# Both down projections of the decoder trunk as seven block products, the first one's weight sums built by transfers

## The chip, the core and the metric

The kernel runs on one core of a Trainium2 chip. The time is the device time of one execution in microseconds (us). Three runs of the kernel before took 1356.61, 1356.44 and 1354.90 us, median 1356.44. The profiled execution took 1356.42 us.

## What is computed

A decoder trunk of two layers on 512 positions of width 1024, float32. Layer 0 mixes with a convolution and a gated part, layer 1 with dilated attention over 3 x 8 heads. Each layer ends with a feed-forward part. Every matrix product is made of three: both operands are split into a high and a low float32r part, and high x high, high x low and low x high are summed.

```python
def swiglu(x, w_gate, w_up, w_down):
    return (jax.nn.silu(x @ w_gate) * (x @ w_up)) @ w_down
...
        x = layer_norm(DN_ALPHA * x + swiglu(x, ffn_w_gate[layer], ffn_w_up[layer], ffn_w_down[layer]),
                       ln_g[layer, 1], ln_b[layer, 1])
```

The hidden width is 2816, or 22 tiles of 128. The change is in the last product, 512 x 2816 by 2816 x 1024.

## The kernel before, in words

**Stages.** Layer 0: convolution part (0 to 158 us), up projection (158 to 384.5), down projection (384.5 to 506). Layer 1: attention (506 to 1012), up projection (to 1240), down projection (to 1345.5), last norm. The queues of the five engines are written out by hand, and semaphores are waited for in that order.

**Slabs.** Weights come in slabs of 128 x 1024 floats (512 KB). SyncE (SP) loads slab s into slot s % 4 of `stage` (L598) once the low part of slab s - 4 is made. ScalarE (ACT) rounds it to `w_hi` (`split_high`, L1401) once TensorE (PE) has used slab s - 4. GpSimd (POOL, `split_low`, L707) or VectorE (DVE, `low_slab`, L2323) makes `w_lo`, and PE follows.

**Up projections.** The last 20 hidden tiles ("units") are made by seven half-size products in place of eight. Each unit takes a slab of gate and a slab of up weights. DVE adds blocks of them (`sum31` L2239, `sum2` L2248, `sum4` L2254) and makes all low parts. The up slab of unit n is loaded (SP L649) once DVE has made the low part of the last operand of the unit two before (`low_d`, L2282), and `sum31` waits for it. The unit's turn ends with `corner_12` (L2301), the Silu on ACT (L1655) and `unit_hidden` (L2309), which writes a row of `ht`. POOL has nothing to do here.

**Down projection of layer 0.** Plain: 22 slabs, each 4 token tiles x 2 halves x 3 matmuls of 512 columns, 528 in all (L846 to L848). ACT splits weights and `ht` rows (`high_ht`, L1664), POOL makes the weights' low part, DVE the rows' (`low_ht`, L2316). Between them DVE works out the rotary angles (`rotary_angles` 0 to 3, behind rows 8 to 11, in the tile `gate`), and ACT the sine and cosine tables (`rotary_tables`, L1572, behind row 14). PE ends with `finish_tiles`, which goes tile by tile over the last three slabs, so that the norm of tile 0 begins three tiles before the end.

**Down projection of layer 1.** By blocks (`down_by_blocks`). The 22 hidden tiles are 11 pairs. For each pair PE does four products of 6 matmuls with two prepared slabs from DRAM (`t_rows`: 22 slabs), then with two plain slabs, six slabs of "four" sums (five whole, one half), and nine plain ones: 264 + 132 + 66 = 462 matmuls. DVE makes sums and low parts (`sums_of` L2335 and L2338, `fourth_sum`, `low_sums` L2350, `low_own` L2356, `low_row`, `corners`). The norm of tiles 0 and 1 begins behind the "four" slabs, with the last six plain slabs put between its steps (`between`).

**Sums of weights.** `t_rows` is built in DRAM during attention. Behind every fourth slab SP copies three pieces per pair (`copy_blocks`, 1.25 MB), and POOL issues four accumulating transfers per pair (`block_sums`: step 0 L782, 1 L785, 2 L789, 3 L792), one behind each `split_low`.

**Seam.** `norm` (ACT L1422, L1427, L1435; DVE L1943, L1963; POOL `add_shift` L715) makes x of each tile, PE turns it (`turn_x`, L860), ACT and DVE split it, and the next stage's columns begin (`columns_behind_norm`). The lines that the change touches stand below.

Of the kernel before, what the change touches and what calls it, by code (L numbers as in the profile page):

```python
# [7 lines left out]
F32 = mybir.dt.float32  # L8
# [3 lines left out]
ALU = mybir.AluOpType  # L12
# [31 lines left out]
N_IN, N_OUT, N_UP, N_DOWN, N_ATT = 16, 8, 2 * KF, KF, 72  # L44
# [8 lines left out]


PAIRS = KF // 2
FRONT_ROWS = 2
SUM4_SLABS = (PAIRS + 1) // 2
S_REST = S_DOWN1 + 2 * PAIRS
S_SUM4 = S_REST + FRONT_ROWS
S_ROWS = S_SUM4 + SUM4_SLABS  # L60
N_SLABS = S_ROWS + PAIRS - FRONT_ROWS
OP_SLOTS = 4
# [14 lines left out]
HT_RING = 9  # L77
# [38 lines left out]
def trunk(nc, x, positions, ev_w_in, ev_conv_w, ev_conv_b, ev_conv_ln_g, ev_conv_ln_b, ev_sgu_ln_g,  # L116
# [3 lines left out]
    with ctx:  # L120
# [49 lines left out]
        with ExitStack() as s:  # L170
# [13 lines left out]
            def ht_rows(k):  # L184

                slot = k % HT_RING
                if slot < HT_FIRST:
                    return hr_hi[:, slot, :], hr_lo[:, slot, :]
                n, half = divmod(slot - HT_FIRST, 2)
                chunks = slice(2 * half, 2 * half + 2)  # L190
                return tuple(t[:, n, chunks, :].rearrange("p k n -> p (k n)") for t in (xs_hi, xs_lo))

# [27 lines left out]
            rot_tmp = gate[:, 0, :].rearrange("p (n t) -> p n t", n=4)  # L220
            pos_i = ones[:, :].bitcast(I32)
        with ExitStack() as s:
# [22 lines left out]
            t_rows = nc.dram_tensor("t_rows", (2 * PAIRS + SUM4_SLABS, P, SLAB), F32, kind="Internal").ap()  # L245
# [103 lines left out]
        t_copied = sem("t_copied")  # L349
        t_two = sem("t_two")  # L350
        t_three = sem("t_three")
        t_four = sem("t_four")
        h_sum_set = sem("h_sum_set")
        h_four_set = sem("h_four_set")
        op_hi_set = sem("op_hi_set")
        op_lo_set = sem("op_lo_set")
        m_done = sem("m_done")
        m_kept_set = sem("m_kept_set")
        corner_set = sem("corner_set")
# [160 lines left out]

        def row_blocks(slab):

            if S_SUM4 <= slab < S_ROWS:
                q = slab - S_SUM4
                return ht[:, 4 * q + 1:min(4 * q + 4, KF):2, 0:HALF]
            return pair_blocks(row_pair(slab))[:, 0:4:3, :]

        def slab_width(slab):  # L530

            return SLAB // 2 if slab == S_ROWS - 1 else SLAB

        def row_pair(slab):

            return slab - S_REST if slab < S_SUM4 else slab - S_ROWS + FRONT_ROWS

        def slab_view(slab):
# [31 lines left out]
            if S_DOWN0 <= slab < S_ATT:  # L570
                return rows(ffn_w_down[0], slab - S_DOWN0)
# [2109 lines left out]
```

## Time and profile before

| what | value |
|---|---|
| median of 3 runs | 1356.44 us |
| profiled execution | 1356.42 us, span of instructions 1354.6 us |
| PE busy | 1341.0 us (99%) |
| DVE busy | 940.1 us (69%) |
| ACT busy | 642.9 us (47%) |
| POOL busy | 435.1 us (32%) |
| granted clock of PE | 0.997 of full speed |
| moved by DMA | 176.23 MB, mean 130 GB/s |

Busy time and idle time are told apart by semaphore events. Matmuls are pipelined: one of 512 columns is shown as 0.39 us long, and the next starts 0.23 us behind it, so the time of a stage is the number of matmuls by that step, plus stalls. The 1.8 us between execution and span lie before the first and behind the last instruction.

### The profile page before, as it was taken

To read this page: it belongs to the slowest core of one execution; us is meant where nothing else is said; L and a number is where in the kernel's file an instruction comes from. 1 tells how busy PE (TensorE), PEld (TensorE's weight loads), DVE (VectorE), ACT (ScalarE), POOL (GpSimd) and SP (SyncE) were. 2 spreads that over 40 slices of the span, in tenths; PEclk is the share of its full clock that TensorE was granted. 3 is DMA by queue.
4 is the path that set the end of the run, shared out by engine and by line. 5 is a ranking of instruction groups with operands and counts; after the bars stand their busy time and mean duration, and the time that the engine had idled before them with its cause. 6 is when DMAs were issued, how large, how long until landed. Compare 5 with 4: busy or idle time off the path is not lost.

```text
span 1354.6 us, 20715 instructions
## 1 busy us (share of the span) xinstructions
PE 1341.0 (99%) x8055; PEld 1195.8 (88%) x8055; DVE 940.1 (69%) x1219; ACT 642.9 (47%) x997; POOL 435.1 (32%) x240
## 2 busy tenths in 40 slices
PE   8999999999999999999999999999999999999997
PEld 7887899999988889888888888888889999999885
DVE  3997598888866456777542767644238888889977
ACT  4465555554543343333422334333446455556566
POOL 4785600000054445555544535354242000000002
PEclk9999999999999999999999999999999999999999
DMA  9322224334353325777375776545222434335653
GB/s 272 93 95 85 71 68 120 93 102 115 95 176 105 94 62 162 193 189 187 95 218 147 178 191 164 130 142 148 55 62 76 112 93 113 103 93 202 202 181 123
DMA packets 197083, 176.23 MB, mean 130 GB/s; under 512 B 10293, under 2 KB 163657, under 8 KB 196840
## 3 DMA queue, kind: packets, MB, share of 16 engines
q1 hardware_dynamic: 182648, 156.59, 38.7%
q0 software_dynamic: 7744, 14.42, 6.1%
q10 hardware_dynamic: 6624, 4.29, 1.3%
q8 instruction: 45, 0.74, 0.2%
q14 instruction: 22, 0.18, 0.0%
HBM read 171.04 MB, written 33.08 MB: 151 GB/s over the span
## 4 chain that ended last, share of the span: by engine, by line
PE 97%; ACT 1%; DVE 1%; DMA 1%; issue 0%; SPq 0%; DVEq 0%; ACTq 0%
PE pq L1135 10%; PE pq L1134 10%; PE pq L1132 10%; PE pq L824 9%; PE pq L825 9%; PE pq L826 9%; PE pq L846 8%; PE pq L847 8%; PE pq L848 8%; PE pq L1330 3%; PE pq L1328 3%; PE pq L1329 3%; PE pq L1307 1%; PE pq L1266 1%; PE pq L1279 1%; PE pq L1300 1%
## 5 line engine op out<-in xcount | busy, mean ns | idle before, releaser
L707 POOL TENSOR_TENSOR w_lo<-stage,w_hi 128x1024 fp32r<-128x1024 f32 x132 | 327.0, 2482 | 573.5 <-ACT w_hi L1401 573.5
L1401 ACT ACTIVATE w_hi<-stage 128x1024 fp32r<-128x1024 f32 x173 | 179.1, 1053 | 199.4 <-PE pq L848 126.3
L824 PE MATMUL pq<-xt_hi,w_hi 128*128 128x512 f32 (+1 forms) x624 | 228.4, 366 | 0.5 <-DVE xt_lo L1930 0.4
L826 PE MATMUL pq<-xt_hi,w_lo 128*128 128x512 f32 (+1 forms) x624 | 225.2, 361 | 0.0
L825 PE MATMUL pq<-xt_lo,w_hi 128*128 128x512 f32 (+1 forms) x624 | 225.2, 361 | 0.0
L1134 PE MATMUL pq<-xt_lo,w_hi 128*128 128x256 f32 x632 | 178.9, 283 | 0.0
L1135 PE MATMUL pq<-xt_hi,w_lo 128*128 128x256 f32 x632 | 178.9, 283 | 0.0
L1132 PE MATMUL pq<-xt_hi,w_hi 128*128 128x256 f32 x632 | 178.8, 283 | 0.0
L715 POOL TENSOR_TENSOR x_res<-x_res,norm_b 128x512 f32<-128x512 f32 x24 | 30.4, 1292 | 338.7 <-ACT x_res L1435 337.2
L824 PEld LDWEIGHTS pq<-xt_hi,w_hi 128*128 128x128 f32 x624 | 117.9, 189 | 19.6 <-DVE xt_lo L1930 1.2
L826 PEld LDWEIGHTS pq<-xt_hi,w_lo 128*128 128x128 f32 x624 | 117.8, 189 | 18.0
L1132 PE MATMUL pq<-xs_hi,w_hi 128*128 128x256 f32 x472 | 133.6, 283 | 0.0
L1134 PE MATMUL pq<-xs_lo,w_hi 128*128 128x256 f32 x472 | 133.6, 283 | 0.0
L1135 PE MATMUL pq<-xs_hi,w_lo 128*128 128x256 f32 x472 | 133.6, 283 | 0.0
L825 PEld LDWEIGHTS pq<-xt_lo,w_hi 128*128 128x128 f32 x624 | 117.9, 189 | 17.1
L1132 PEld LDWEIGHTS pq<-xt_hi,w_hi 128*128 128x128 f32 x632 | 121.3, 192 | 0.1
L1134 PEld LDWEIGHTS pq<-xt_lo,w_hi 128*128 128x128 f32 x632 | 121.3, 192 | 0.1
L1135 PEld LDWEIGHTS pq<-xt_hi,w_lo 128*128 128x128 f32 x632 | 121.3, 192 | 0.0
L1132 PEld LDWEIGHTS pq<-xs_hi,w_hi 128*128 128x128 f32 x472 | 90.6, 192 | 0.0
L1134 PEld LDWEIGHTS pq<-xs_lo,w_hi 128*128 128x128 f32 x472 | 90.6, 192 | 0.0
L1135 PEld LDWEIGHTS pq<-xs_hi,w_lo 128*128 128x128 f32 x472 | 90.6, 192 | 0.0
L2540 DVE TENSOR_TENSOR qk<-qk,norm_g 32x1024 f32<-32x1024 f32 x24 | 85.6, 3566 | 0.8
(287 smaller groups left out, 2915.7 us busy)
## 6 DMA issues: line engine op xcount, KB each, us to landing
stage<-in_od_w_qkv_dram SPq DMA_DIRECT2D x72, 512.0 KB, 4.4
stage<-in_ffn_w_gate_dram SPq DMA_DIRECT2D x44, 512.0 KB, 4.9
stage<-in_ffn_w_up_dram SPq DMA_DIRECT2D x44, 512.0 KB, 4.0
stage<-in_ffn_w_down_dram SPq DMA_DIRECT2D x33, 512.0 KB, 3.5
stage<-t_rows SPq DMA_DIRECT2D x27, 512.0 KB, 3.3
t_rows<-in_ffn_w_down_dram SPq DMA_DIRECT2D x22, 512.0 KB, 7.4
stage<-in_ev_w_in_dram SPq DMA_DIRECT2D x16, 512.0 KB, 5.5
t_rows<-in_ffn_w_down_dram POOLq DMA_DIRECT2D x11, 512.0 KB, 7.9
```

The costliest lines, as they stand in the source:

```text
L707: pool.tensor_tensor(w_lo[slab % RING][:, :], w_stage[slab % RING][:, :], w_hi[slab % RING][:, :].bitcast(F32), ALU.subtract).then_inc(w_l ...
L824: pe.matmul(o, hi[:, k, :], x_hi, start=(k == 0), stop=False)
L825: pe.matmul(o, hi[:, k, :], x_lo, start=False, stop=False)
L826: last = pe.matmul(o, lo[:, k, :], x_hi, start=False, stop=(k == KD - 1))
L846: pe.matmul(o, t_hi[:, tile * P:(tile + 1) * P], hi, start=first, stop=False, skip_group_check=resumed)
L847: pe.matmul(o, t_hi[:, tile * P:(tile + 1) * P], lo, start=False, stop=False, skip_group_check=resumed)
L848: return pe.matmul(o, t_lo[:, tile * P:(tile + 1) * P], hi, start=False, stop=end, skip_group_check=resumed)
L1132: pe.matmul(o, hi[:, k, :], x_block[0][:, k, :], start=(first and k == 0), stop=False, skip_group_check=True)
L1134: pe.matmul(o, hi[:, k, :], x_block[1][:, k, :], start=False, stop=False, skip_group_check=True)
L1135: last = pe.matmul(o, lo[:, k, :], x_block[0][:, k, :], start=False, stop=(k == KH - 1), skip_group_check=True)
L1401: act.activation(w_hi[slab % RING][:, 0:width], w_stage[slab % RING][:, 0:width], ACT.Copy).then_inc(w_hi_ready, 1)
L2540: dve.tensor_tensor(rows, rows, rot[0:ROT, :, :], ALU.add).then_inc(qk_set, 1)
```

## The change

The down projection of layer 0 goes by `down_by_blocks` too, with 462 matmuls in place of 528. Semaphores of the scheme get a copy per layer, and so does `t_rows`. Its copies stand on SP behind slabs 8 to 23 of the convolution part, its accumulating transfers on POOL behind slabs 17 to 23 and then two per unit of the up projection. The "four" sums take seven slabs (four whole, three half) in both layers. POOL makes no low parts in layer 0's down projection, DVE makes all. The rotary work moves: angles behind pairs 5 and 9 and behind the third and sixth "four" slab, tables behind the second of the last nine slabs, in a tile of their own (`rot_tmp`). In the norm, `split(0)` moves behind `between(1)`.

```diff
+SUM4_WHOLE = 4
+SUM4_SLABS = PAIRS - SUM4_WHOLE
+SUMS_FROM = 16
+COPY_BEHIND = (8, 9, 11, 12, 14, 15, 17, 18, 20, 21, 23)
...
+            def copy_blocks(layer, j):
+
+                upper, lower, both, own, four = block_rows(layer, j)
+                if j >= 2:
+                    sp.wait_ge(t_copied[layer][j % 2], 48 * (j // 2))
...
             for slab in range(RING + 4, S_UP0):
                 load(slab)
+                if slab in COPY_BEHIND:
+                    copy_blocks(0, COPY_BEHIND.index(slab))
...
+            def load_down(first, layer, e):
+                for n in range(N_DOWN):
+                    if n == 2:
+                        load_ln(e, layer, 1)
+                    if n < D_REST and n % 2 == 0:
+                        sp.wait_ge(t_three[layer], 16 * (n // 2 + 1))
+                    elif n == D_SUM4:
+                        sp.wait_ge(t_four[layer], 16 * PAIRS)
+                    load(first + n)
...
+            sums_begun = 0
             for slab in range(S_UP0):
                 split_low(slab)
+                if slab >= SUMS_FROM:
+                    block_sums(0, sums_begun)
+                    sums_begun += 1
                 if slab == 17:
                     pool.wait_ge(acc_set, 1)
...
-            feed_forward(S_DOWN0, 1)
+            for u in range(UNITS):
+                pool.wait_ge(s31_set, min(u + 2, UNITS))
+                for _ in range(2):
+                    if sums_begun < 4 * PAIRS + 4:
+                        block_sums(0, sums_begun)
+                        sums_begun += 1
+            pool.wait_ge(w_lo_ready, plain(S_ATT))
+            norm(1, S_ATT)
...
                         if r:
                             last.then_inc(w_used, 1)
+                            if layer == 0 and slab < end_slab - 1:
+                                turn_x(2, slab - end_slab + 3)
...
-                split(0)
+                if not between:
+                    split(0)
                 squares_of(0)
...
                 if between:
                     between(1)
+                    split(0)
                     scale(0)
...
+                for slab in range(fours, row_slabs + 4):
+                    high_row(slab)
+                    if layer == 0 and slab == row_slabs + 1:
                         rotary_tables()
...
+                        if layer == 0 and j in (5, 9):
+                            rotary_angles(j // 9)
...
+                        if layer == 0 and slab - fours in (2, 5):
+                            rotary_angles(2 + (slab - fours) // 5)
```

**How the queues change.** POOL in the convolution part, slabs 16 to 18. `tap_sum` and `acc` are the partial and whole sums of the convolution, `L707` and `L730` the low part of a slab. Before:

```order
L755 TENSOR_TENSOR tap_sum<-tap_sum,mixed 128x512 x2
L707 TENSOR_TENSOR w_lo<-stage,w_hi 128x1024
L747 TENSOR_TENSOR tap_sum<-acc 128x512
L755 TENSOR_TENSOR tap_sum<-tap_sum,mixed 128x512 x2
L760 TENSOR_TENSOR acc<-acc,tap_sum 128x512
```

Now:

```order
L730 TENSOR_TENSOR w_lo<-stage,w_hi 128x1024
L778 DMA t_rows<-in_ffn_w_down_dram 256x1x512
L796 TENSOR_TENSOR tap_sum<-acc 128x512
L804 TENSOR_TENSOR tap_sum<-tap_sum,mixed 128x512 x2
L809 TENSOR_TENSOR acc<-acc,tap_sum 128x512
L730 TENSOR_TENSOR w_lo<-stage,w_hi 128x1024
L782 DMA t_rows<-in_ffn_w_down_dram 128x512
```

A transfer of step 1 is issued ahead of the last sums of the convolution.

ACT at the end of layer 0's down projection. Rows that write `w_hi` split a weight slab, rows that write `hr_hi` or `xs_hi` its partner from `ht`. The rows `ht,sq_sum` and `std` are the norm's squares and root, `x_res` its scaled tile. Before:

```order
L1401 ACTIVATE w_hi<-stage 128x1024
L1422 ACTIVATE ht,sq_sum<-pq,neg_mean 128x1024
L1427 ACT_TABLE_LOAD
L1427 ACTIVATE std<-sq_sum,eps 128x1
L1435 ACTIVATE x_res<-pq,rstd 128x512 x2
```

Now:

```order
L1594 ACTIVATE sin_t<-rot_tmp 32x128 x4
L1594 ACTIVATE cos_t<-rot_tmp 32x128 x4
L1421 ACTIVATE w_hi<-stage 128x1024
L1709 ACTIVATE hr_hi<-ht 128x512
L1421 ACTIVATE w_hi<-stage 128x1024
L1709 ACTIVATE xs_hi<-ht 128x512
L1442 ACTIVATE ht,sq_sum<-pq,neg_mean 128x1024
L1447 ACT_TABLE_LOAD
L1447 ACTIVATE std<-sq_sum,eps 128x1
L1421 ACTIVATE w_hi<-stage 128x1024
L1709 ACTIVATE xs_hi<-ht 128x512
```

Behind these come the second tile's squares, three more pairs of splits, one more `w_hi`, and only then `x_res`. The tables stand seven slabs before the end, where there was nothing of them.

DVE at pair 5 of layer 0's down projection. `w_lo<-stage` is `low_slab`, the rows from `sums` and `ht` into `xs_lo` are `low_sums` and `low_own`. Now:

```order
L2313 TENSOR_TENSOR w_lo<-stage,w_hi 128x1024
L2340 TENSOR_TENSOR xs_lo<-sums,xs_hi 128x768
L2346 TENSOR_TENSOR xs_lo<-ht,xs_hi 128x256
L2148 CAST rot_tmp<-ones 128x128
L2150 TENSOR_SCALAR rot_tmp<-rot_tmp,cst 128x128
L2134 TENSOR_SCALAR rot_tmp<-rot_tmp 128x128
L2136 TENSOR_SCALAR rot_tmp<-rot_tmp 128x128
L2138 TENSOR_SCALAR rot_tmp<-rot_tmp 128x128
L2142 SCALAR_TENSOR_TENSOR rot_tmp<-rot_tmp 128x128 x3
L2155 TENSOR_SCALAR rot_tmp<-rot_tmp 128x128
L2313 TENSOR_TENSOR w_lo<-stage,w_hi 128x1024
```

In layer 1's block version the last row follows `low_own` at once.

## Rows read from the trace of the kernel before

**Rows 1.** The page, its part on the chain that ended last, by engine
```profile
PE 97%; ACT 1%; DVE 1%; DMA 1%; issue 0%; SPq 0%; DVEq 0%; ACTq 0%
```

**Rows 2.** Busy time by stretch; columns: stretch, length, PE, PEld, DVE, ACT, POOL, clock, DMA
```profile
384.50:506.10 121.60, 121.58 (x544) 100.39 (x543) 65.37 (x74) 45.87 (x67) 55.94 (x25) 1.00 0.31 96
...
1240.00:1345.50 105.50, 105.44 (x464) 86.25 (x462) 91.33 (x128) 67.49 (x93) 4.34 (x4) 1.00 0.52 173
```

**Rows 3.** Timeline of PE; columns: start, length, engine, line, operation, idle before
```profile
499.28 0.39 PE L846 MATMUL pq<-w_hi,xs_hi 128*128 128x512 f32 x1
...
501.09 0.39 PE L848 MATMUL pq<-w_hi,hr_lo 128*128 128x512 f32 x1
...
506.24 0.36 PE L824 MATMUL pq<-xt_hi,w_hi 128*128 128x256 f32 x1 [0.16 <-issue]
...
1345.19 0.39 PE L848 MATMUL pq<-w_hi,xs_lo 128*128 128x512 f32 x1
```

**Rows 4.** Timeline of DVE, layer 0's down projection (415 to 419) and layer 1's
```profile
415.83 0.21 DVE L2153 CAST gate<-ones 128x128 f32<-128x128 int32 x1
...
418.17 0.23 DVE L2160 TENSOR_SCALAR gate<-gate 128x128 f32<-128x128 f32 x1
...
1265.50 0.42 DVE L2356 TENSOR_TENSOR xs_lo<-ht,xs_hi 128x256 fp32r<-128x256 f32 x1
...
1270.02 0.95 DVE L2350 TENSOR_TENSOR xs_lo<-sums,xs_hi 128x768 fp32r<-128x768 f32 x1
```

**Rows 5.** Timeline of ACT, layer 0's tables and layer 1's last rows
```profile
450.86 1.73 ACT L1572 ACTIVATE sin_t<-gate 32x128 f32<-32x128 f32 x4
...
1319.84 1.06 ACT L1401 ACTIVATE w_hi<-stage 128x1024 fp32r<-128x1024 f32 x1 [1.14 <-PE pq L848]
...
1326.90 1.04 ACT L1401 ACTIVATE w_hi<-stage 128x1024 fp32r<-128x1024 f32 x1
```

**Rows 6.** Timeline of POOL, PE and DVE at the two norms
```profile
489.12 2.40 POOL L707 TENSOR_TENSOR w_lo<-stage,w_hi 128x1024 fp32r<-128x1024 f32 x1 [3.03 <-ACT w_hi L1401]
497.45 2.55 POOL L715 TENSOR_TENSOR x_res<-x_res,norm_b 128x512 f32<-128x512 f32 x2 [5.93 <-ACT x_res L1435]
...
501.32 1.03 PE L860 MATMUL pq<-ident,x_res 128*128 128x128 f32 x8
...
1338.95 1.28 DVE L1963 SCALAR_TENSOR_TENSOR pq<-pq,neg_mean,norm_g 128x1024 f32<-128x1024 f32 x1
```

**Rows 7.** Timeline of POOL and PE in the convolution part
```profile
103.36 1.30 POOL L747 TENSOR_TENSOR tap_sum<-acc 128x512 f32<-128x512 f32 x1
...
107.48 1.27 POOL L760 TENSOR_TENSOR acc<-acc,tap_sum 128x512 f32<-128x512 f32 x1
...
107.94 1.99 PE L965 MATMUL pq<-acc,ones 128*128 128x512 f32 x4
```

**Rows 8.** Timeline of SP, DVE and ACT, one unit of layer 0's up projection
```profile
251.83 0.37 SPq L649 DMA_DIRECT2D stage<-in_ffn_w_up_dram  x1
...
255.85 1.22 DVE L2239 TENSOR_TENSOR sums<-stage 128x1024 f32<-128x1024 f32 x1
...
258.27 0.63 ACT L1655 ACTIVATE gate<-gate 128x512 f32<-128x512 f32 x1 [1.51 <-DVE gate L2301]
...
259.46 0.69 DVE L2309 TENSOR_TENSOR ht<-pq,gate 128x512 f32 x1 [1.22 <-PE pq L1135]
```

**Rows 9.** Slab loads (L598) of attention issued at 599.4, then at 635.5
```profile
DMA to landing us min/median/max: 5.1/5.1/5.1
...
DMA to landing us min/median/max: 4.2/4.2/4.2
```

**Rows 10.** Timeline of POOL and DVE in attention
```profile
596.75 2.65 POOL L707 TENSOR_TENSOR w_lo<-stage,w_hi 128x1024 fp32r<-128x1024 f32 x1
599.09 1.32 POOL L785 DMA_DIRECT2D t_rows<-in_ffn_w_down_dram  x1
...
596.79 3.70 DVE L2540 TENSOR_TENSOR qk<-qk,norm_g 32x1024 f32<-32x1024 f32 x1
```

More of the change, by code:

```diff
@@ L76 @@
 HT_FIRST = 3
-HT_RING = 9
 C_FAR, C_NEAR, C_UT, C_FREQ, C_SIGN = 0, 256, 640, 768, 769
@@ L650, in load_up @@
                                      gate_up[j % 2][:, :, 2 * t + j // 2, :]).then_inc(w_loaded[slot], 16)
-            def load_down(first, layer, e, end):
-                if layer:
-                    sp.wait_ge(t_four, 16 * PAIRS)
-                load(first)
-                load(first + 1)
-                load_ln(e, layer, 1)
-                for slab in range(first + 2, end):
-                    load(slab)
+            def load_down(first, layer, e):
[7 more added lines that the diff above has]
+                    load(first + n)
             load_up(S_UP0, 0)
@@ L1774, in feed_forward @@
-                high_ht(1)
                 split_high(down + 1)
                 split_high(down + 2)
-                high_ht(2)
                 unit_gate(last, last % 2)
+                high_sums(1)
+                high_own(1)
                 split_high(down + 3)
-                for k in range(HT_FIRST, KF):
-                    high_ht(k)
-                    if RING <= k + 1 < KF:
-                        split_high(down + k + 1)
-                    if layer == 0 and k == 14:
+                for j in range(2, PAIRS):
+                    split_high(down + 2 * j)
+                    split_high(down + 2 * j + 1)
+                    high_sums(j)
+                    high_own(j)
@@ new lines, in feed_forward @@
+                for slab in range(rest, fours):
+                    high_row(slab)
+                for n, (dst, bank) in enumerate(((sums, 1), (gate, 5))):
+                    act.wait_ge(m_done[layer], n + 1)
+                    for r in range(2):
+                        last = act.activation(dst[:, r, :], pq[:, bank + 2 * r, :], ACT.Copy)
+                    last.then_inc(m_kept_set[layer], 1)
+                for slab in range(fours, row_slabs + 4):
+                    high_row(slab)
+                    if layer == 0 and slab == row_slabs + 1:
@@ L1785, in feed_forward, with between @@
                         rotary_tables()
-                norm(e, down + N_DOWN)
+                def between(n):
+                    for slab in ((row_slabs + 4, row_slabs + 5), range(row_slabs + 6, end_slab))[n]:
+                        high_row(slab)
+                norm(e, down + N_DOWN, between)
             feed_forward(0, S_UP0, S_DOWN0, 1)
@@ L2445, in unit_step @@
                         sum2(u + 2, par)
-                    elif layer:
+                    else:
                         sums_of(0)
-                        low_slab(S_DOWN1)
+                        low_slab(down)
                         low_sums(0)
-                    else:
-                        low_d(u + 1, 1 - par, static + 1)
-                        low_ht(0)
                     corner_12(u, par)
-                    if layer and not more:
+                    if not more:
                         low_d(u + 1, 1 - par, static + 1)
@@ L2484, in feed_forward @@
                     unit_step(u, u % 2, u)
[L2485 to L2500 removed]
+                down_by_blocks()
+            feed_forward(0, S_UP0, S_DOWN0, 1)
             def stream_tables():
```

374 lines of the change are left out of this document (154 added, 220 removed).

## The prediction

> **What bounds the kernel now.** I read the chain that ended last first. It lies on PE for 97% [rows 1]. The table by stretch says the same of both down projections: PE is busy 121.58 of 121.60 us in layer 0 (with its seam) and 105.44 of 105.50 in layer 1, at full clock [rows 2]. So a matmul taken away shortens the time, as long as nothing else comes late. What may come late is read from timelines of the other queues, each against the moment at which PE needs the result. The steps of PE are 0.2265 us, (501.09 - 499.28) / 8 [rows 3].
>
> The sum is made against the profiled execution, 1356.42 us. The median of the three runs is 1356.44, so the two stand together. No change means within 0.2%, or 2.7 us.
>
> **Term 1, matmuls: -15.0.** 528 become 462, 66 x 0.2265 = 14.95 us. Nothing else on PE is taken away. The turns of tiles 0 and 1 stay.
>
> **Term 2, the usual small stalls: +0.4.** Layer 1's block version runs from 1240.0 to 1345.19 + 0.23 = 1345.42 [rows 2, 3], 105.4 us for 462 steps of 104.6, so 0.8 of stalls. The plain version had 121.74 (384.5 to 506.24) less 119.6 less 1.8 for the turns, 0.3. The difference is 0.4 to 0.5.
>
> **Term 3, rotary angles on DVE: +0.3 (0 to 2.5).** DVE now makes all low parts. In layer 1 a pair takes it 4.87 us (steps of 1.14 twice, 0.87, 0.72 and 0.33 three times) of PE's 5.44, so it gains 0.57 per pair until ACT holds it. Part 0 takes 2.57 us, 415.83 to 418.17 + 0.23 [rows 4]. Put behind pair 5 (`low_own` ends at 1265.9), it moves pair 6's `low_sums` from 1270.97 to about 1273.1. PE wants pair 6 at 1240.4 + 6 x 5.44 = 1273.0. With 0.15 us from DVE to PE that is a stall of 0.3. Part 1 (2.05) comes when 1.6 of lead is won back, and pair 10 has no next sum, so it is hidden. Parts 2 and 3 (2.25 each) find 1 us of lead or more. Without any lead each part would be paid in full for a slab, hence 2.5.
>
> **Term 4, the tables on ACT: +3.3 (0 to 5).** Sine and cosine are two times 1.73 us [rows 5]. Before, ACT had two splits, about 1.6 us, against the 24 steps or 5.44 us that PE took for a slab there, and the gaps hid them. Call the nine plain slabs at the end p0 to p8. In layer 1 ACT begins p2 at 1319.84, waiting for PE, and p4 at 1326.90, behind the first squares [rows 5]. PE needs p4 at 1345.4 less 36 steps less two slabs of 2.72, 1331.8, and the split takes 2.9 to be ready on DVE, so there are 1.9 us of room. Now p1 starts at 1318.4 (three half slabs let PE free its slot 1.3 later), then 1.5 for p1 and 3.5 for the tables: p2 at 1323.4, 3.6 late. The norm's first sum on DVE, the squares and the table load for the root follow, and p4 begins at 1330.9, 4.0 late against 1.9 of room. Rolled on to p8 by the same durations, PE waits 0.3, 0.4, 1.4, 0.4, 0.1, 0.4 and 0.4, together 3.3. The lower end is zero (another 2 us of room somewhere), the upper one 3.5 and the second squares.
>
> **Term 5, the seam: +2.7 (0 to 5).** Before, the adds of tile 0 end at 497.45 + 2.55 = 500.0, and PE turns it at 501.32, 1.3 later [rows 6]. Now tile 0's gain stands behind the low parts of p8, as at 1338.95 in layer 1, 6.5 us before the end [rows 6]. Count from R, the end of p8's low parts. PE has 12 matmuls until the first turn, R + 2.9. The chain is the last rotary step 0.45, gain 1.2, scale 0.7, then POOL. But POOL has `split_low` of attention's first slab first, 2.4 us [rows 6], to about R + 3.0, and two adds, 2.55, bring it to R + 5.5. PE can turn the first half meanwhile. It waits 2.0 at tile 0, 0.3 at tile 1 and 0.4 at the first columns. The lower end is the old seam, the upper one both tiles in full.
>
> **Term 6, the convolution part: +1.1 (0 to 1.3).** POOL's last sums run without a gap from 103.36, and the last one ends at 107.48 + 1.27 = 108.75. PE takes two `ones` matmuls in 107.94 to 109.86, so the second starts at 108.9, just behind it [rows 7]. A transfer of step 1 now stands ahead of these sums. POOL spends 1.32 us on one such beside DVE work [rows 10]. I take 1.1, and 0 if POOL had unseen room. The later six transfers fall where POOL idles. The eleven copies on SP stand ahead of slab loads that PE wants only three slabs later, 3 x 24 steps or 16 us, which covers a load that has to queue.
>
> **Term 7, layer 0's up projection: +3.3 (0 to 15).** POOL idles here, but two accumulating transfers per unit now share the DMA engines with the slab loads, and one load stands in a loop with no depth. The up slab is issued at 251.83 and `sums` starts at 255.85, 4.0 later; the Silu ends at 258.27 + 0.63 = 258.9; the hidden row could start at 259.0 and starts at 259.46, held by PE [rows 8]. The room is 0.45 us per unit of 10.08 (84 steps of half size, 0.12 each). In attention a slab load issued beside steps 0 and 1 landed after 5.1 us, and one beside steps 2 and 3 after 4.2 [rows 9], against 4.0. So units take turns at +1.1 and +0.2: 0.65 over the room, then 0.25 won back, 0.4 per two units. Nine pairs give 3.6, less 0.3 before PE feels it. If transfers add under 0.45 everywhere it is 0. The upper end is the rival below.
>
> The skill states a mechanism for the same sharing. The Trainium skill, DMA: Bandwidth & Descriptors, section SWDGE vs HWDGE vs iDMA, says that inside each DMA engine transfers issued by GpSimd and by SP lie in different queues, and that the engine takes turns between them. By that rule a load beside a steady accumulate could take up to twice its transfer time, which is the strong case below, and the 5.1 us say it is milder.
>
> **Term 8, layer 1: +0.5 (0 to 1).** Seven "four" slabs in place of six delay the last rows by 0.3, and the last norm, which ended 0.7 behind PE, by 0.2 more.
>
> **Hidden:** the new splits of DVE (POOL's former ones), by the idle time that layer 1 shows: 91.33 of 105.50 busy [rows 2]. The start of the down projection: it is layer 1's queue, and the sums of pair 0 are there 100 us earlier.
>
> **Sum:** -15.0 + 0.4 + 0.3 + 3.3 + 2.7 + 1.1 + 3.3 + 0.5 = -3.4, and 1356.4 - 3.4 = **1353.0 us**. Own range of this case 1349 to 1356.5.
>
> **Rivals.**
>
> *A, most of it is kept.* Layer 1's twin runs with 0.8 us of stalls, so terms 4, 5 and 7 might shrink to little. With all three at 0 the time is 1343.7, with each at a half 1348.4. For it speaks rows 2, against it the queue positions worked out above.
>
> *B, the load loop decides, slower.* Place: the up slab's load between `low_d` and `sum31`. If the load takes 1.5 us more beside steps 0 and 1 and 0.6 beside 2 and 3, two units cost 1.05 + 0.15, nine pairs 10.8, term 7 is 10.5 and the time 1360.2; with 1.8 and 0.9 it is 1365.6. It decides from a mean of about 1.0 us added per load (term 7 over 9.4). For it: our transfers are already in flow when the load starts, 3 to 4 us behind their issue, and two follow at once. Against it: 5.1 and 4.2 [rows 9].
>
> *C, POOL's issuing holds DVE.* 1.32 + 0.8 us per unit against 1.6 of idle time on DVE would cost 0.5 per unit, 10 us in all, on top of the sum: 1363. Against it speaks attention: the split of POOL runs from 596.75 to 599.40, the DVE operation beside it ends at 596.79 + 3.70 = 600.49, 1.1 after the split, though the transfer is being issued in just that time (599.09 to 600.41) [rows 10]. So the split holds DVE, the issue doesn't. The Trainium skill, SBUF — State Buffer, section Who interferes with whom, says that a DVE instruction with two SBUF inputs contends with a GpSimd one that reads SBUF, and not with one that only writes. By that rule, the trace agrees.
>
> *D, a wait on `t_three` or `t_four` stops the loads.* The last sums are issued a unit before the end and land within 8 us; the first slab needs only pair 0. Its price would be a landing, 8 us.
>
> **How the numbers follow.** Forecast 0.45 (faster 0.27, same 0.14, slower 0.04), A 0.28 (all faster), B 0.18 (slower 0.12, same 0.06), C 0.04 (slower), D 0.05 (same). Faster 0.55, same 0.25, slower 0.20, with C, D and both tails rounded. The range 1344.5 to 1361 leaves out the best of A and the worst of B and C.
>
> **What the profile after would show.** Right: 66 fewer matmuls of 512 columns; PE with gaps of a few tenths to 1.4 us in the last six slabs of layer 0's down projection, released by DVE low parts; about 2 us at the first turn, released by POOL; about 1 us ahead of the last `ones` matmul; units of 10.2 to 10.4 us in place of 10.08 in layer 0 alone. Wrong: units still 10.08 (A) or over 10.6 (B); DVE operations in the units longer than 1.22 and 0.69 (C); a gap of several us at the start of the down projection (D).

## The result, and the profile after

The changed kernel is slower: 1374.24 us against 1356.44, ratio 1.0133 (95% interval 1.0104 to 1.0162). The forecast was 1353.0, range 1344.5 to 1361. The profiled execution took 1373.06 us with a span of 1371.0, 16.4 more than before.

The page of the changed kernel has this for the chain that ended last, by engine, which answers to [rows 1]:

```profile
PE 79%; DMA 5%; DVE 5%; POOL 4%; issue 4%; ACT 2%; DVEq 0%; SPq 0%; POOLq 0%; ACTq 0%
```

PE had 97% of the chain before and has 79% now. What is new in it is told by its list of longest pieces (start, length, what):

```profile
200.86 4.70 DMA stage<-in_ffn_w_up_dram
211.26 6.24 DMA stage<-in_ffn_w_up_dram
...
234.31 7.09 DMA stage<-in_ffn_w_up_dram
...
507.10 2.53 DVE sin_t L2175
```

These are slab loads of layer 0's up projection, of about 4 us before, and the rotary sign product at the seam. The table by stretch (columns as in [rows 2]) has the up projection, one piece of it, and layer 0's down projection with its seam:

```profile
182.30:403.90 221.60, 208.34 (x1682) 206.41 (x1681) 167.94 (x223) 108.32 (x163) 33.62 (x38) 0.98 0.72 157
337.00:340.40 3.40, 3.40 (x16) 3.40 (x17) 3.24 (x4) 1.77 (x4) 0.00 (x0) 0.52 0.96 122
403.90:520.50 116.60, 111.25 (x480) 88.46 (x478) 103.17 (x167) 73.86 (x108) 7.73 (x5) 0.99 0.53 177
```

The same matmuls, 84 per unit in 20 units, took 201.6 us before, at a DMA share of 0.40. PE is idle in this stretch for 13.3 us, and in places its clock is granted at half. From starts of matmuls in both timelines the 16.4 us come out as follows:

| stretch | before | after | difference |
|---|---|---|---|
| start, to the first columns | 16.53 | 14.88 | -1.65 |
| first columns to the first unit | 166.21 | 167.39 | +1.18 |
| layer 0's up projection | 201.59 | 221.61 | +20.02 |
| its down projection, seam and columns, to attention's first product | 152.37 | 147.11 | -5.26 |
| attention to layer 1's up projection | 501.70 | 501.67 | 0.0 |
| layer 1's up projection | 201.60 | 201.59 | 0.0 |
| layer 1's down projection, to the last matmul | 105.19 | 105.31 | +0.1 |
| behind the last matmul | 9.41 | 11.44 | +2.03 |

The first row is scatter as far as is known: this start took 14.5 to 17.1 us in the profiles of the changed kernel and its variants, and 16.6 in a second one of the kernel before.

So the products were saved where they should be, and the up projection gave back more than all of it. The waits of that stretch, longest of each kind:

```profile
DVE sums L2235 <- DMA stage<-in_ffn_w_up_dram: 26.2, 16, 3.5
...
PE pq L1164 <- DVE ht L2305: 13.3, 9, 2.4
```

The first difference of a unit (`sum31`) waits for the up slab's load in 16 units, the hidden row is late behind it, and PE stands in nine of them. What such a stand costs is seen in PE's timeline:

```profile
242.65 0.28 PE L1167 MATMUL pq<-xt_hi,w_lo 128*128 128x256 f32 x1
245.38 0.58 PE L1164 MATMUL pq<-xt_hi,w_hi 128*128 128x256 f32 x1 [2.45 <-DVE ht L2305]
245.75 0.42 PE L1166 MATMUL pq<-xt_lo,w_hi 128*128 128x256 f32 x1
245.97 0.42 PE L1167 MATMUL pq<-xt_hi,w_lo 128*128 128x256 f32 x1
```

The next start comes 2.73 us later in place of 0.12, and then the steps are 0.21 for some 3 us. The row of the stretch at 337.0 above shows the same behind another such gap: granted clock 0.52, that is the lower level of 1.2 GHz. The nine gaps add up to 14.7 us beyond a step, and the slow steps behind them to 5.3, mostly behind three gaps of 2.3 to 2.6 us: the 20 us.

### The profile page after: what moved, and what is told of

Read it like the earlier page. It is cut to its first block, busy times and chain, and to the rows that moved or that the text cites. A ratio compares the mean times of both kernels' runs of the same rounds, so it can differ in the third digit from the quotient of the medians.

```text
span 1371.0 us, 20908 instructions
## 1 busy us (share of the span) xinstructions
PE 1336.6 (97%) x7989; PEld 1187.5 (87%) x7989; DVE 986.4 (72%) x1320; ACT 669.3 (49%) x1039; POOL 417.7 (30%) x262
## 3 DMA queue, kind: packets, MB, share of 16 engines
q1 hardware_dynamic: 190312, 179.67, 43.1%
## 4 chain that ended last, share of the span: by engine, by line
PE 79%; DMA 5%; DVE 5%; POOL 4%; issue 4%; ACT 2%; DVEq 0%; SPq 0%; POOLq 0%; ACTq 0%
PE pq L850 8%; PE pq L852 8%; PE pq L851 8%; PE pq L1164 7%; PE pq L1166 7%; PE pq L1167 7%; PE pq L872 6%; PE pq L874 6%; PE pq L873 6%; DMA stage<-in_ffn_w_up_dram 5%; PE pq L1348 3%; PE pq L1350 3%; PE pq L1349 3%; POOL tap_sum L804 2%; POOL w_lo L730 1%
## 5 line engine op out<-in xcount | busy, mean ns | idle before, releaser
L730 POOL TENSOR_TENSOR w_lo<-stage,w_hi 128x1024 fp32r<-128x1024 f32 x110 | 271.4, 2472 | 419.6 <-ACT w_hi L1421 306.8
L1421 ACT ACTIVATE w_hi<-stage 128x1024 fp32r<-128x1024 f32 (+1 forms) x192 | 197.1, 1042 | 163.7 <-PE pq L874 88.1
L1164 PE MATMUL pq<-xt_hi,w_hi 128*128 128x256 f32 x632 | 182.0, 288 | 13.3 <-DVE ht L2305 13.3
L851 PEld LDWEIGHTS pq<-xt_lo,w_hi 128*128 128x128 f32 x624 | 117.9, 189 | 17.1
L2313 DVE TENSOR_TENSOR w_lo<-stage,w_hi 128x1024 fp32r<-128x1024 f32 (+1 forms) x80 | 94.5, 1181 | 18.1 <-ACT w_hi L1421 17.6
L872 PE MATMUL pq<-w_hi,xs_hi 128*128 128x512 f32 x228 | 90.4, 396 | 1.5 <-DVE xs_lo L2357 0.9
```

The costliest lines, as they stand in the source:

```text
L730: pool.tensor_tensor(w_lo[slab % RING][:, :], w_stage[slab % RING][:, :], w_hi[slab % RING][:, :].bitcast(F32), ALU.subtract).then_inc(w_l ...
L851: pe.matmul(o, hi[:, k, :], x_lo, start=False, stop=False)
L872: pe.matmul(o, t_hi[:, tile * P:(tile + 1) * P], hi, start=first, stop=False, skip_group_check=resumed)
L1164: pe.matmul(o, hi[:, k, :], x_block[0][:, k, :], start=(first and k == 0), stop=False, skip_group_check=True)
L1421: act.activation(w_hi[slab % RING][:, 0:width], w_stage[slab % RING][:, 0:width], ACT.Copy).then_inc(w_hi_ready, 1)
L2313: dve.tensor_tensor(w_lo[slab % RING][:, 0:width], w_stage[slab % RING][:, 0:width], w_hi[slab % RING][:, 0:width].bitcast(F32), ALU.subtr ...
```

## The experiments

All ratios stand against the kernel before, measured on the same chip as the run (1354.7 to 1355.1 us there; 1356.4 where the change was measured). Stretches are of the one profiled execution. In runs 1, 2 and 5 sums of weights stay unfinished, so the slabs' waits for them are left out in runs 1 and 2.

**1. No transfers in the up projection.** My first theory was the forecast's rival B: transfers and loads share the DMA engines.

```diff
-            for u in range(UNITS):
-                pool.wait_ge(s31_set, min(u + 2, UNITS))
-                for _ in range(2):
-                    if sums_begun < 4 * PAIRS + 4:
-                        block_sums(0, sums_begun)
-                        sums_begun += 1
...
+                    if layer == 0 and n == 0:
...
+                        sp.wait_ge(t_two[0], 64)
...
```

> Leaves out the 40 accumulating transfers of the first layer's up projection (its weight sums stay unfinished, so the output is another one); the 8 places in the convolution part, all copies and the whole down projection stay as in the changed kernel. The load theory (the transfers share the DMA engines with the two 512 KB loads of each unit, the loads land late, PE idles 14.7 us at the units' ends and runs some 5 us longer at half clock after the longest of these gaps) expects the up stretch back at 201.6 us instead of 221.6 and 1354.2 us in all, ratio to the kernel before 0.998. The rival, that the loss sits in the down projection and the norm behind it and the up stretch is only where it shows in one profile, expects less than 5 us back: 1369 or more.

Measured: 1352.82 us, ratio 0.9982 (0.9973 to 0.9992), up stretch 201.59. The whole loss of that stretch hangs on these transfers.

**2. One small transfer per unit, at the same point.**

```diff
-                for _ in range(2):
-                    if sums_begun < 4 * PAIRS + 4:
-                        block_sums(0, sums_begun)
-                        sums_begun += 1
+                if u < 18:
+                    upper, _, _, own, _ = block_rows(0, 2 + u // 2)
+                    at = slice(512 * (u % 2), 512 * (u % 2) + 512)
+                    pool.dma_start(own[:, at], upper[:, at], accum_op=ALU.add).then_inc(t_three[0], 16)
```

> In each of 18 units of the first up projection one accumulating transfer of 256 KB in place of two of 256 and 512 KB (the others are left out, so sums stay unfinished and the output is another one), issued at the same point, where the unit's first difference is done. The load theory: 256 KB land about 5.2 us after the issue, the next loads are issued 4.3 us after it, so the transfer is nearly out of their way: up stretch 201.6 to 204, 1354 to 1357 us in all. A rival, that it is POOL's issuing (0.8 to 1.1 us each, beside DVE's operations) which makes DVE late and the loop long, keeps half of the loss with half of the issues: up stretch about 211, total about 1364.

Measured: 1352.62 us, 0.9987 (0.9977 to 0.9997), up stretch 201.59. Half the issues cost nothing, so POOL's issuing as such is not it. This run changes both the number of issues and the bytes; it is the next that changes neither.

**3. The transfers together with the loads.**

```diff
-                pool.wait_ge(s31_set, min(u + 2, UNITS))
+                pool.wait_ge(d_lo_set, u + 1)
```

> All transfers as in the changed kernel, but POOL waits for the unit's d split instead of its first difference, so that both transfers of a unit are issued together with its two loads and not 4.3 us ahead of them. The load theory expects a worse kernel: every load now runs beside a fresh 512 to 768 KB, landings of 7 us and more in every unit instead of some, up stretch 230 to 250 us, total 1382 to 1403. If only the volume counts, or the issuing, the stretch stays at 221 and the total at 1374.

Measured: 1353.34 us, 0.9994 (0.9985 to 1.0004), up stretch 201.59. My theory was wrong in its core: with every transfer kept, and every load beside them, the loss is gone. Volume alone doesn't decide either; the DMA share of this stretch is 0.73 and PE is never idle:

```profile
181.90:383.50 201.60, 201.60 (x1682) 201.60 (x1681) 168.03 (x223) 108.36 (x162) 33.56 (x38) 1.00 0.73 170
```

The rows of the large transfer of step 1 (L778) and of the up slab's load behind or ahead of it (L679) say why. First of the changed kernel, where the load goes out 3.6 us behind the transfer:

```profile
L778 POOL DMA_DIRECT2D t_rows<-in_ffn_w_down_dram x1: 1370/1370/1370, 207.7 to 207.7; - x1
DMA to landing us min/median/max: 8.1/8.1/8.1
...
L679 SPq DMA_DIRECT2D stage<-in_ffn_w_up_dram x1: 373/373/373, 211.3 to 211.3; - x1
DMA to landing us min/median/max: 6.2/6.2/6.2
```

Then of run 3, where it goes out 0.8 us ahead of it (and 0.3 us ahead of the smaller transfer of step 0):

```profile
L778 POOL DMA_DIRECT2D t_rows<-in_ffn_w_down_dram x1: 1367/1367/1367, 211.4 to 211.4; - x1
DMA to landing us min/median/max: 9.5/9.5/9.5
...
L679 SPq DMA_DIRECT2D stage<-in_ffn_w_up_dram x1: 373/373/373, 210.7 to 210.7; - x1
DMA to landing us min/median/max: 4.1/4.1/4.1
```

The load lands as if alone, and the transfer is the one to wait, 9.5 us in place of 8.1. It ends at 220.9, when the next up load is just going out (220.7). The second load of the pair, issued 0.6 to 0.9 us behind the first, now lands after 6.8 to 8.8 us, and before after 5.0; it is wanted later, and PE never waits for it.

The two queues, from run 3's view of 210.5 to 214 us, show what the 0.3 us are worth (packets, MB, share of the 16 engines; `hardware_dynamic` are SP's transfers, `software_dynamic` POOL's):

```profile
q1 hardware_dynamic: 1144, 0.58, 56.5%
q0 software_dynamic: 1, 0.00, 0.3%
```

More than a whole slab of 512 KB has passed while POOL's transfers, issued at 210.9 and 211.4, have moved one packet.

**4. The transfers just ahead of the loads.** New theory: who comes first. Its opponent: only the amount left in flight counts.

```diff
-                pool.wait_ge(s31_set, min(u + 2, UNITS))
+                pool.wait_ge(hid_set, u + 2)
```

> All transfers as in the changed kernel; POOL waits for the unit's hidden product, so that they go out about 1.4 us ahead of the next unit's load, where the changed kernel sends them 4.3 us ahead and the run at the loads 0.3 us behind it. The run at the loads took the loss away (up stretch 201.59 us), against my first theory of shared engines. Theory of who comes first: a load that finds transfers in the queues ahead of it is late, one that leads them lands as if alone. It expects the load to land after 6 us or more in every unit and an up stretch of 221 to 245, total 1373 to 1397. Theory of the tail: the load only shares with what is left of transfers, and POOL's start and descriptors take some 2 us first, so that 1.4 us ahead is as good as together: up stretch 201.6 to 206, total 1353 to 1358.

Measured: 1414.77 us, 1.0443 (1.0425 to 1.0460), up stretch 260.99. The same transfers, 1.7 us earlier relative to the load than in run 3, cost 59 us. The unit loads of both slabs together (L679) from 190 to 400 us, in the changed kernel, in run 3 and in run 4 (who waited for them: total us and times; then their landings):

```profile
  DVE sums L2235: 26.2, 16
...
DMA to landing us min/median/max: 4.0/5.4/7.9
```

```profile
  DVE sums L2235: 1.2, 5
...
DMA to landing us min/median/max: 3.8/4.1/8.8
```

```profile
  DVE sums L2235: 51.8, 16
...
DMA to landing us min/median/max: 6.4/8.0/9.3
```

For the up slab alone, which is the one that `sum31` waits for, the medians are 4.0 us in the kernel before, 5.3 in the change, 3.9 in run 3 and 7.7 in run 4. So a load behind fresh transfers takes nearly twice its time, and one that leads them by 0.3 us takes none of it. That is the same sharing in both orders, as run 3's second load shows with its 6.8 to 8.8 us: what is protected is a load whose data is on its way before POOL's transfer is. How the two share shows in the queues of run 4 from 219 to 222 us:

```profile
q0 software_dynamic: 202, 0.41, 78.7%
q1 hardware_dynamic: 437, 0.22, 32.4%
```

POOL's packets hold the engines for most of the time, and the loads move 0.22 MB in these 3 us, where loads alone moved 0.84 (253 to 256 us of the kernel before).

**5. Just ahead, with plain copies.** Run 4 with this in all four transfers:

```diff
-accum_op=ALU.add
+accum_op=ALU.add if layer else ALU.bypass
```

> The run with the transfers 1.4 us ahead of the loads (1414.8 us, up stretch 260.99), with plain copies of the same bytes by POOL's queue in place of the accumulating transfers of the first layer (its sums are not built, so the output is another one). If bytes in front of a load in the queues are the cause, whatever they do at their end, the first layer's up stretch stays at 240 to 261 and the total at 1395 to 1415. If the accumulation's read and write of the target are what holds the engines, the copies are out of the way in half the time: up stretch 202 to 225, total 1355 to 1380.

Measured: 1386.07 us, 1.0235 (1.0219 to 1.0250), up stretch 234.24. In between the two, and in neither range: the copy of step 1 lands after 4.8 us where the accumulating one took 8.3, but the loads of both slabs still take 6.6 (median; 8.0 in run 4), and 33 of the 59 us remain. So both count. A little over half of the loss is there with any bytes ahead of the load. The rest goes with the accumulation, which keeps the engines longer: the 0.79 MB of steps 0 and 1 took 43.1% of the 16 engines over 12 us in run 4, 5.2 us, and 27.4% over 10 us as plain copies, 2.7 us.

**6. Behind the loads.** On the kernel of run 10 below.

```diff
-                pool.wait_ge(d_lo_set, u + 1)
+                pool.wait_ge(s12_lo_set, min(u + 2, UNITS))
```

> The best kernel so far (1346.6 us, up stretch 201.67) with its up transfers issued at the next split on DVE, some 1.4 us later: behind the load of the unit by 1.7 us. The larger transfer landed 9.5 us after its issue at the loads, 0.2 us before or after the next load went out. The theory of who comes first expects that nothing changes as long as the rest in flight at the next load is small, and a first sign of harm at this shift: that load finds about 1 us of transfers left in every second unit; up stretch 201.6 to 206, total 1346.5 to 1351. Unharmed down to 201.6 would say that the remainder of a transfer does not matter, only a fresh one does.

Measured: 1347.34 us, 0.9943 (0.9928 to 0.9958), up stretch 201.91 against 201.67. One gap of 0.23 us behind a load of 4.9 us, the first sign of harm, at the low end of what was expected. The transfers now go out 1.4 us behind the load (211.16 against 209.75). So a microsecond late is nearly free, and a microsecond early is not.

**7. The rotary work elsewhere, transfers as in the change.** Angles behind pairs 3, 5, 7 and 9, tables behind the last pair, the sign product behind the norm.

```diff
-                        if layer == 0 and j in (5, 9):
-                            rotary_angles(j // 9)
+                        if layer == 0 and j in (3, 5, 7, 9):
+                            rotary_angles((j - 3) // 2)
...
-                        if layer == 0 and n:
-                            rotary_angles(4)
                     norm(e, between)
+                    if layer == 0:
+                        rotary_angles(4)
```

> The changed kernel with its rotary work moved: the four parts on DVE behind pairs 3, 5, 7 and 9, the eight Sin activations on ACT behind the last pair (before the row slabs), and the sign product (2.61 us beside POOL's split in the profile of the change) behind the whole norm. In the first down projection the changed kernel loses 8.3 us against the second layer's same products and 2.4 us more at the turns. My theory, that ACT's table load and eight activations among the plain slabs (3.0 us of PE waits) and the sign product that POOL's split holds up (3.1 us, then slow-clock products 2.2 us) are the cause, expects 6 to 9 us back: 1365 to 1368 us. The rival, that the seam is late because DVE and ACT now both work off slab splits behind each other there whatever stands beside them, expects under 3 us back: 1371 or more. A mishap would be parts of the angles among the pairs making PE wait there by about 0.3 us each.

Measured: 1367.53 us, 1.0092 (1.0075 to 1.0108), 6.7 less than the change, of which the ratios, 1.0092 against 1.0133, keep 5.6, and their intervals touch. In the profile, down and seam fell only from 147.11 to 144.04, and the up stretch was 0.9 longer. So 3.1 us are shown for this edit; the profiled execution, 1371.02, was the slowest of four, and where the rest lies no trace shows. The PE waits at the plain slabs went and that at tile 0 shrank from 3.1 to 0.6, but four waits of 0.6 to 1.4 us came up among the pairs: there the angles find no lead on DVE. That mishap was larger than expected.

**8. Transfers at the loads, and the sign product behind the norm.**

```diff
-                        if layer == 0 and n:
-                            rotary_angles(4)
                     norm(e, between)
+                    if layer == 0:
+                        rotary_angles(4)
```

> The kernel with the transfers at the loads (1353.3 us), and the sign product behind the whole norm. Theory: in the slow run of the change the product ran 2.61 us beside POOL's split and 0.5 us alone; the wait of PE for the normed tile 0 (3.1 us), the slow-clock products behind it (about 1.0 us) and part of the later turns hang on it. Expected: down and seam 147.5 to between 142.5 and 144.5, total 1348 to 1351. Rival: the tables' activations and the split of the next slab on POOL already make the tile late: less than 2 us back, 1351.5 or more.

Measured: 1349.39 us, 0.9955 (0.9939 to 0.9972); down and seam 143.06 against run 3's 147.49, of which 1.0 is a gap at the third pair that run 3 alone shows. Timelines of the seam, of the changed kernel and of this run:

```profile
506.58 2.76 POOL L730 TENSOR_TENSOR w_lo<-stage,w_hi 128x1024 fp32r<-128x1024 f32 x1 [112.71 <-DVE w_lo L2313]
507.02 2.61 DVE L2175 TENSOR_SCALAR sin_t<-sin_t,cst 32x512 f32<-32x512 f32 x1
...
511.87 1.26 POOL L738 TENSOR_TENSOR x_res<-x_res,norm_b 128x512 f32<-128x512 f32 x1 [2.53 <-ACT x_res L1455]
...
513.19 0.66 PE L886 MATMUL pq<-ident,x_res 128*128 128x128 f32 x4 [2.97 <-POOL x_res L738]
```

```profile
486.70 2.79 POOL L730 TENSOR_TENSOR w_lo<-stage,w_hi 128x1024 fp32r<-128x1024 f32 x1 [104.24 <-DVE w_lo L2313]
487.14 1.28 DVE L1958 SCALAR_TENSOR_TENSOR pq<-pq,neg_mean,norm_g 128x1024 f32<-128x1024 f32 x1
...
490.79 0.66 PE L886 MATMUL pq<-ident,x_res 128*128 128x128 f32 x4 [0.42 <-POOL x_res L738]
```

The sign product ended 0.3 us behind POOL's split, not after its own 0.5 us (0.47 in the kernel before, with no split beside it). In this run it stands later, begins at 506.10 beside the next split, which ends at 506.61, and ends at 506.89: again 0.3 us behind the split. The gain, PSUM to PSUM with one operand in SBUF, is not held by the same split: 1.28 us. The tile comes 2.5 us earlier, and the slow-clock matmuls behind the long wait go with it.

**9. Angles and tables earlier.** Behind the first and third "four" slab, tables behind the fifth.

```diff
-                        if layer == 0 and slab - fours in (2, 5):
-                            rotary_angles(2 + (slab - fours) // 5)
+                        if layer == 0 and slab - fours in (0, 2):
+                            rotary_angles(2 + (slab - fours) // 2)
...
-                    if layer == 0 and slab == row_slabs + 1:
+                    if layer == 0 and slab == fours + 4:
```

> The kernel of the run before, and the last two parts of the angles behind the first and third of the four-sums slabs, the eight Sin activations behind the fifth (before: behind the third and sixth, and ten slabs in). Theory: there ACT and DVE are slabs ahead of PE, and the 2.3 us of PE waits at the plain slabs go: total 1.5 to 2.5 us below the run before it. Rival: ACT has no more lead there than later, because the work-off of four-sums slabs is as tight, and the waits only move: within 0.7 us of the run before it.

Measured: 1348.59 us, 0.9945 (0.9929 to 0.9962); 0.8 below run 8, with executions of the two overlapping, and down and seam 142.16, 0.9 less. Waits of 0.3, 0.3, 1.1 and 0.3 became one of 1.08, which run 11 takes up. Between the two expectations.

**10. Transfers behind the tap sums, the last fourth sums in the down projection.**

```diff
-                if slab >= SUMS_FROM:
-                    block_sums(0, sums_begun)
-                    sums_begun += 1
                 if slab == 17:
...
+                if slab >= SUMS_FROM:
+                    block_sums(0, sums_begun)
+                    sums_begun += 1
             norm(0, S_UP0)
...
+            for n, late in enumerate(range(4 * 7 + 3, 4 * PAIRS + 4, 4)):
+                pool.wait_ge(w_lo_ready, plain(S_DOWN0 + 4 + 3 * n) + 1)
+                block_sums(0, late)
```

> The kernel of the run before, and two moves of transfers: in the convolution part each stands behind the slab's tap sums on POOL in place of ahead of them (theory: the third mean product's wait of 1.1 us goes), and the last five of the fourth sums go out in the down projection behind slabs 4, 7, 10, 13 and 16, so that the up projection ends three units without transfers (theory: PE's wait of 1.2 us at the third pair, which stands only in the run with the transfers at the loads, goes). Expected in all 1.5 to 2.5 us below the run before it. Rival: transfers in the down projection meet its own loads there and PE waits: same or more.

Measured: 1346.59 us, 0.9936 (0.9919 to 0.9952), 2.0 below run 9 and 8.5 below the kernel before. The convolution part is back at 166.24 us from 167.37, and down and seam are at 141.71, 0.45 less. The late sums cost nothing: the gap that they were to cure stood in run 3's profile only. This is the best version.

**11. Angles behind the corner sums.** On the kernel of run 10.

```diff
-                        if layer == 0 and slab - fours in (0, 2):
-                            rotary_angles(2 + (slab - fours) // 2)
+                        if layer == 0 and slab - fours in (3, 5):
+                            rotary_angles(2 + (slab - fours - 3) // 2)
...
-                    if layer == 0 and slab == fours + 4:
+                    if layer == 0 and slab == fours + 6:
```

> The best kernel so far (1346.6 us) with the last two parts of the angles behind the fourth and sixth of the four-sums slabs, the Sin activations behind the seventh. In that kernel's trace one PE wait of 1.05 us is left behind the first parts, where DVE has just come out of 3.8 us of corner sums and is behind already. If that is its cause, the wait goes and the time is 1345.6 (0.5 to 1.2 less); if the Sin table and the activations on ACT set it, it moves along with them and the time stays at 1346.6.

Measured: 1346.55 us, 0.9943 (0.9929 to 0.9956). The total says that the wait moved along with the tables, 1.05 us at 452.8 before and 1.08 at 464.8 now. The timelines say that these are two waits of about one size. First run 10, then this run:

```profile
450.82 1.22 DVE L2318 TENSOR_TENSOR w_lo<-stage,w_hi 128x1024 fp32r<-128x1024 f32 x1
451.96 0.68 DVE L2362 TENSOR_TENSOR hr_lo<-ht,hr_hi 128x512 fp32r<-128x512 f32 x1
...
452.83 1.74 ACT L1599 ACTIVATE sin_t<-rot_tmp 32x128 f32<-32x128 f32 x4
```

```profile
459.96 1.75 ACT L1599 ACTIVATE cos_t<-rot_tmp 32x128 f32<-32x128 f32 x4 [0.20 <-DVE rot_tmp L2177]
...
461.74 1.06 ACT L1426 ACTIVATE w_hi<-stage 128x1024 fp32r<-128x1024 f32 x1
...
462.83 1.23 DVE L2318 TENSOR_TENSOR w_lo<-stage,w_hi 128x1024 fp32r<-128x1024 f32 x1 [1.97 <-ACT w_hi L1426]
```

In run 10 the wait was over when the first table began, and DVE had not idled from the corner sums on: these to 447.0, then a pair of low parts, the angles from 448.66 to 450.91, and the next pair. DVE set it, as the first theory had it, and it went. In its place came one that ACT sets: two tables of 1.75 us ahead of the next split, for which DVE idles 1.97 us.

**12. The kernel before, once more,** with no edit.

> The kernel before, once more, for what a stretch of one profile is worth. Behind its last product it showed 9.4 us to the end of the span, the changed kernel 11.4, and its descendants 10.1 to 11.6; their last stores land within the same 2.7 and 3.0 us. If the change makes these 2 us, this profile shows 9.4 again; if it is scatter, anything up to 11.5. The start (first column product of 256 at 16.5 us before, 13.5 to 16.1 in the others) should show scatter too. The stretches in between should agree within 0.1 us: up 201.6, down and seam 152.4, attention 501.7.

Measured: 1356.61 us, span 1354.8. Up 201.59, down and seam 152.38, attention 501.70, and 9.44 us behind the last matmul. So these stretches are good to 0.1 us, and the 2.0 us at the end are the change's. The start was 16.6 us again, so this profile doesn't show its scatter; the variants do.

## Why the prediction was wrong

**Term 1, -15.0: right.** 66 matmuls are gone (516 to 450 up to the first turn), and the stretch is 14.96 shorter by them.

**Term 7, +3.3: wrong, +20.0.** This is what decided. The mechanism and the place were right, and rival B named them: the up slab's load in the loop. The step that failed is the price of a load, "1.1 and 0.2" from [rows 9]. Those loads stood in another order to their transfers. In attention the load of 599.4 goes out 0.3 us behind step 1 (POOL at 599.09) and 3.3 behind step 0. Here both transfers had gone out 3.6 to 4.5 us ahead and were in full flow, and the up slabs' loads took 4.5 to 7.1 us beside steps 0 and 1 (median 6.4, the first unit's 4.0 aside) and 4.1 to 5.4 beside 2 and 3 (median 4.8). I had written this down, "our transfers are already in flow when the load starts", and then weighed it less than the rows of the other phase. The distance counts within this too: beside steps 0 and 1 a load took 6.2 to 7.1 us where step 1 had gone 3.6 or 3.7 us ahead, 4.5 to 6.1 at 4.0, and 4.0 in the one unit where it had gone 5.8 ahead. By B's own formula such landings (2.4 and 0.8 added) give 2.3 per two units, or 21 us; PE lost 14.7. The second part that failed is that no term had the clock: the steps behind the gaps, about 3 us of them at half clock in each of three places, cost 5.3 us. Even B's larger case, 1365.6 us, fell short of the 1374.2.

The Trainium skill, DMA: Bandwidth & Descriptors, section SWDGE vs HWDGE vs iDMA, has the DMA engine take turns between the queues of GpSimd's and SP's transfers. That a load takes up to twice its time by it was my estimate. The trace agrees with the estimate in run 4, 7.7 us against 4.0, though not by even shares: while both flowed, the loads moved about a quarter of what they move alone. I called it the strong case and took the mild one.

**Terms 3 and 4, +0.3 and +3.3: about right.** Against layer 1's same products layer 0 had lost 0.35 us by the plain slabs and 3.35 by the last six matmuls before the turn, so the tables cost 3.0. The waits were 0.3, 0.3, 1.1, 0.3, 0.2 and 0.3, and the trace of the change shows the chain of ACT named for them: tables from 484.35 to 487.9, then the split, for which DVE idles 2.9 us. They went when the tables stood earlier (runs 7 and 9).

**Term 5, +2.7: too small, about +6.** All of down and seam lost 9.7 (15.0 less 5.3), less 0.5 for term 2, 0.35 and 3.0. Counted directly, from the last matmul before the first turn to attention's first product, it is 41.1 us against 35.6, 5.5 more. The step that failed is "the last rotary step 0.45": it lasted 2.61, beside the very split that the term put there. I had the fact in hand, since rival C told of a DVE operation that a split of POOL held, and didn't apply it here. The wait behind it was 3.1 in place of 2.0, and the clock fell after it too (steps of 0.43 in place of 0.23).

**Term 6, +1.1: right.** +1.18, a wait of 1.03 us ahead of the third `ones` product, released by the tap sums on POOL; run 10 took it away.

**Term 2, +0.4: right in kind, a little small.** Layer 0 pays what layer 1 pays, 0.8 us up to the first turn, where the plain version had 0.1.

**Term 8, +0.5: +2.1, mostly open.** The products of layer 1 took 0.1 more. Behind the last matmul came 2.0: the last DVE operation of the norm is 0.7 later, and the rest lies behind the last stores, which land after the same 2.7 and 3.0 us. Run 12 shows that it is no scatter. The end follows the number of transfers that POOL issues: from the last store's landing to the end of the span it is 0.4 us with 44 (before) and 50 (run 1), 0.8 with 68 (run 2), and 1.8 to 1.9 with the 88 of the change and all others. It isn't the second set of semaphores or the larger `t_rows`, which run 1 has too, and not layer 0's accumulation, which run 5 lacks. How the transfers lengthen the end isn't shown.

**Rivals.** A fell in the up projection, though its spirit came true once the transfers were moved: 1346.6 us. C is refuted by run 3, where the same issues on POOL cost nothing, and by the changed kernel's own trace: `sum31` and `unit_hidden` last 1.22 and 0.69 us in the units, as before. D didn't happen; no load waited on `t_three` or `t_four` noticeably. The chances were the real fault: with B's argument "for" unanswered, 0.18 was too low.

## What to carry to other kernels

A background transfer is priced first by where it stands against the load that something waits for, and by its bytes only where it is ahead; the share of busy DMA engines says nothing of it. Issue it just behind that load, and let it be done, or nearly, before the next one. If a landing time is taken from another stretch of a trace, take it from a load that stood in the same order and distance to such transfers. A small helper operation placed on DVE beside a POOL split can cost the rest of the split, as the sign product did and the gain did not, so it goes where nothing is queued behind it. And when a wait seems to move with an edit, look up in both timelines what ends it: run 11 took one away and made another of the same size.

## What the runs showed of the hardware that I had not expected

- The same transfers cost 59 us when issued 1.5 us ahead of a 512 KB load, 20 us at about 4 us ahead, nothing at 0.3 us behind it, and 0.2 to 0.3 at 1.4 us behind (up stretches 260.99, 221.61, 201.59 and 201.91).
- An accumulating transfer of 512 KB landed after 8.3 us where a plain copy by the same queue took 4.8 (medians of step 1 in runs 4 and 5); of 256 KB from DRAM, 4.2 against 3.1 (step 2). It kept the 16 engines busy for nearly twice as long per byte.
- While accumulating transfers and loads flowed together, the loads moved 0.22 MB in 3 us against 0.84 alone.
- A gap of PE may cost more than its length. In the changed kernel those of 2.3 to 2.6 us were each followed by 1.4 to 1.6 us lost at 1.2 GHz, those of 1.8 and 1.9 by 0.1. The length alone doesn't decide: in run 4 gaps of 1.9 and 2.0 us were followed by 1.6, and some of 2.8 to 3.7 by 0.1.
- The operation that writes `sin_t`, 32 x 512 with one large operand in SBUF, lasted 0.47 us with no split beside it, and 2.61 or 0.79 us beside one, by how much of the split was left: it ended 0.3 us behind the split each time.
- The end of the program grew from 0.4 to 1.8 us behind the last landing as POOL's transfers went from 44 or 50 to 88.
